# Scan stage of an RWKV block: one transposed product moved behind the next level's first step, and the adaptive weights moved from VectorE to ScalarE and GpSimd

## What is computed

```python
# the scan, per head: S is value x key
S = S * w_t + (S @ a_t) b_t^T + v_t k_t^T ;  y_t = S @ r_t
# the adaptive weights of the second block, which depend on c alone
mod = silu(c) @ ada_w + ada_b          # 1024 x 6144, for sh1, sc1, g1, sh2, sc2, g2
```

## Time and profile before

| | |
|---|---|
| median of 3 runs | 3071.32 us (3067.51 to 3080.73) |
| the profiled execution | 3072.96 us, of which its span (first to last instruction) is 3071.2 us |
| mean granted TensorE clock over the span | 0.981 of full |
| busy over the span | PE 2954.0, PEld 2562.2, DVE 1954.5, ACT 1195.3, POOL 765.9 us |
| the scan | from 242.28 to about 549.5 us in the trace |

### The profile page before, as it was taken

How to read it: one execution, slowest core, us unless ns; L and a number is a source line. 1 busy time by engine, 2 the same in 40 slices (tenths; PEclk the granted TensorE clock), 3 DMA queues, 4 the chain that set the end, 5 groups by cost and what they waited for, 6 DMA issues and landing times.

```text
span 3071.2 us, 48256 instructions
## 1 busy us (share of the span) xinstructions
PE 2954.0 (96%) x19809; PEld 2562.2 (83%) x19809; DVE 1954.5 (64%) x3498; ACT 1195.3 (39%) x1949; POOL 765.9 (25%) x517
## 2 busy tenths in 40 slices
PE   8998888899999999999999999999999999999999
PEld 6776888788888878888787878999999997888887
DVE  5584676633324553332468557798979867878878
ACT  6363332423223342332336333445454543333332
POOL 1010111000000200000012002776767763533422
PEclk9998999999999999999999999999999999999999
DMA  4313222333323323332221122779889899999997
GB/s 125 110 37 98 85 86 94 127 98 97 100 97 117 96 86 99 97 96 96 81 81 36 35 87 82 246 273 320 287 297 312 298 334 368 360 366 343 356 367 257
DMA packets 233371, 539.63 MB, mean 176 GB/s; under 512 B 24816, under 2 KB 91632, under 8 KB 231104
## 3 DMA queue, kind: packets, MB, share of 16 engines
q1 hardware_dynamic: 177280, 375.01, 37.0%
q0 software_dynamic: 37440, 136.36, 12.2%
q10 hardware_dynamic: 18432, 25.17, 2.2%
HBM read 484.02 MB, written 52.46 MB: 175 GB/s over the span
## 4 chain that ended last, share of the span: by engine, by line
PE 82%; DVE 7%; POOL 3%; DMA 3%; ACT 3%; issue 2%; SPq 0%; ACTq 0%; DVEq 0%; POOLq 0%
PE bank L396 23%; PE bank L2942 16%; PE bank L399 16%; PE bank L2511 12%; PE bank L2671 3%; POOL etl L2499 2%; DMA eu<-in_peer_u 2%; PE bank L519 1%; PE bank L811 1%; PE bank L1099 1%; POOL taken L2536 1%; DMA gl<-acts 1%; PE bank L1286 1%; PE bank L1143 1%; PE bank L1168 1%
## 5 line engine op out<-in xcount | busy, mean ns | idle before, releaser
L346 DVE TENSOR_TENSOR wl<-raw,wh 128x1024 fp32r<-128x1024 f32 (+2 forms) x241 | 294.5, 1225 | 643.5 <-ACT wh L331 643.5
L331 ACT CAST wh<-raw 128x1024 fp32r<-128x1024 f32 (+2 forms) x241 | 249.7, 1038 | 657.0 <-PE bank L396 367.4
L2499 POOL TENSOR_TENSOR etl<-eu,eth 128x1024 fp32r<-128x1024 f32 x128 | 316.9, 2478 | 390.5 <-ACT eth L2495 389.3
L2511 PE MATMUL bank<-peerhh,eth 128*128 128x384 f32 x1024 | 349.1, 341 | 10.3 <-POOL etl L2499 9.9
L2511 PE MATMUL bank<-peerhh,etl 128*128 128x384 f32 x1024 | 343.6, 336 | 0.0
L2511 PE MATMUL bank<-peerhl,eth 128*128 128x384 f32 x1024 | 343.4, 335 | 0.0
L2942 PE MATMUL bank<-vsh,coefh 128*128 128x512 f32 x768 | 299.2, 390 | 3.2 <-DVE coefl L3007 2.7
L2942 PE MATMUL bank<-vsh,coefl 128*128 128x512 f32 x768 | 298.8, 389 | 0.0
L2942 PE MATMUL bank<-vsl,coefh 128*128 128x512 f32 x768 | 298.8, 389 | 0.0
L2536 POOL DMA_INDIRECT taken<-in_peer_v,gb x128 | 198.2, 1548 | 310.0 <-DVE y_row L2556 302.8
L2963 ACT CAST vsh<-vb 128x1024 fp32r<-128x1024 f32 x128 | 134.7, 1052 | 193.8 <-PE bank L2942 164.5
(11 more groups left out here) (561 smaller groups left out, 6851.6 us busy)
## 6 DMA issues: line engine op xcount, KB each, us to landing
eu<-in_peer_u SPq DMA_DIRECT2D x128, 512.0 KB
vb<-in_peer_v SPq DMA_DIRECT2D x128, 512.0 KB
raw<-in_ada_w SPq DMA_DIRECT2D x48, 512.0 KB, 4.6
acts<-eg ACTq DMA_DIRECT2D x128, 192.0 KB
coefs<-stage SPq DMA_DIRECT2D x24, 1024.0 KB
gd<-coefs SPq DMA_DIRECT2D x16, 1536.0 KB
gl<-acts SPq DMA_DIRECT2D x128, 192.0 KB
raw<-in_ffn_w_gate SPq DMA_DIRECT2D x44, 512.0 KB, 3.6
```

Source lines behind the costliest of these rows:

```text
L331: act.copy(parts_of(c)[0], raw_of(c)).then_inc(*up("w rounded", c))
L346: dve.tensor_tensor(lo, raw_of(c), hi.bitcast(F32), ALU.subtract).then_inc(*up("w split", c))
L2499: pool.tensor_tensor(Et[j % 3][1], Eu[j % 2], Et[j % 3][0].bitcast(F32), ALU.subtract).then_inc(*up("u split", j))
L2511: t = pe.matmul(b, tb[un][:, k * 128:(k + 1) * 128], peer_h[hn][:, k, 1:4, :], start=k == 0 and i == 0, stop=k == 7 and i == 2)
```

## The change

Four edits, all within the scan.

1. PE's xt step becomes a function of its own. The xt step of half 0 comes after both x steps; that of half 1 comes after the next level's two w steps, ahead of that level's grid product. ACT's copies follow the same order.
2. The products of the adaptive weights go to ACT (`ada_scaled`: 2 per piece, in place in `raw`) and the sums to POOL (`ada_added`: 1 or 2 additions per piece). ACT's are placed one half of a piece after each of levels 1 to 4, and two halves at a time after the low blocks, after the corners, after the next group's first turn, and after the copy of y.
3. On POOL the normalisation of y (`dve_gn`) stands between pieces 6g+1 and 6g+2.
4. The last chunk (ch = 3, g = 6) no longer transposes b and k, which nothing reads there.

```diff
--- before.py
+++ after.py
@@ -1158,6 +1158,9 @@
                 t = pe.matmul(b[side(p), bank, 64 * n:64 * n + 64], part(XTc, w)[at_, c:c + 64],
                               eye(l, w)[at_, cw:cw + 64], start=True, stop=True)
         t.then_inc(*up("scan pe", "x full", g, l, w))
+
+    def pe_level_xt(pe, on_pe, g, l, w):
+        order = CROSS[l - 1] if l > 1 else SIDES[1]
         b, before = banks.take_pair(("xt", g, l, w), ("scan act", "xt new", g, l, w), *([("scan dve", "xt low", g, w)] if l == 5 else []))
         for what in before:
             on_pe.wait_ge(*at(*what))
@@ -1210,7 +1213,7 @@
 
         for g in range(NG):
             ch, gp = divmod(g, 2)
-            if gp == 0:
+            if gp == 0 and ch < 3:
                 for name, src in (("b", aa), ("k", k_)):
                     for half in range(2):
                         b, before = banks.take(("bk", name, ch, half), ("bk", name, ch, half))
@@ -1222,12 +1225,16 @@
             for l in range(1, 6):
                 for w in range(2):
                     pe_level_w(pe, on_pe, g, l, w)
+                if l > 1:
+                    pe_level_xt(pe, on_pe, g, l - 1, 1)
                 if l in TASKS:
                     pe_grids(pe, on_pe, g, TASKS[l])
                 for w in range(2):
                     pe_level_x(pe, on_pe, g, l, w)
+                pe_level_xt(pe, on_pe, g, l, 0)
                 if l in ADAS:
                     total(6 * g + ADAS[l])
+            pe_level_xt(pe, on_pe, g, 5, 1)
             for w in range(2):
                 pe_low(pe, on_pe, g, w)
             b, before = banks.take(("g", g), ("g copied", g))
@@ -1318,6 +1325,24 @@
         for what in DECAYED:
             on_act.wait_ge(*at(*what))
 
+        def xt_new(g, l, w):
+            b = banks.pair(("xt", g, l, w))
+            on_act.wait_ge(*at("scan pe", "xt full", g, l, w))
+            if l < 5:
+                act.copy(part(XTc, w).rearrange("p (b n) -> p b n", b=2), b[:, :, 0:128]).then_inc(
+                    *up("scan act", "xt new", g, l, w))
+            else:
+                act.copy(XTf[0:64, :, 2 * w:2 * w + 2, 0:64], bank_four(b, 0)[0:64]).then_inc(
+                    *up("scan act", "xt new", g, l, w))
+
+        def ada_scaled(n, k):
+            ga, i = divmod(n, 4)
+            c = st.plans["ada", ga][0][2][i]
+            on_act.wait_ge(*at("silu c"))
+            on_act.wait_ge(*at(f"w in {c % 4}", c))
+            act.activation(raw_of(c)[:, k, :], raw_of(c)[:, k, :], ACT.Copy,
+                           scale=silu_c[:, 2 * i + k:2 * i + k + 1]).then_inc(*up("scan act", "ada scaled", n, k))
+
         def squares(g):
             on_act.wait_ge(*at("dve step", "y", g, "centred"))
             act.activation(Sq, Yc, ACT.Square).then_inc(*up("y squares", g))
@@ -1327,28 +1352,29 @@
         on_act.wait_ge(*at("bank full", "bonus", KD - 1))
         for g in range(NG):
             ch, gp = divmod(g, 2)
-            if gp == 0:
+            if gp == 0 and ch < 3:
                 for name, dst in (("b", bkT[ch % 2][0]), ("k", bkT[ch % 2][1])):
                     on_act.wait_ge(*at("bank full", "bk", name, ch, 0))
                     for what in bk_free(ch):
                         on_act.wait_ge(*at(*what))
                     act.copy(dst[:, 0:512], banks["bk", name, ch, 0]).then_inc(*up("bk", name, ch, 0))
             for l in range(1, 6):
+                if l > 1:
+                    xt_new(g, l - 1, 1)
                 for w in range(2):
-                    x, b, rows = banks.pair(("x", g, l, w)), banks.pair(("xt", g, l, w)), slice(0, 128 if l < 5 else 64)
+                    rows = slice(0, 128 if l < 5 else 64)
                     on_act.wait_ge(*at("scan pe", "x full", g, l, w))
-                    act.copy(part(Xc, w).rearrange("p (b n) -> p b n", b=2)[rows], x[rows, :, 0:128]).then_inc(
-                        *up("scan act", "x new", g, l, w))
-                    on_act.wait_ge(*at("scan pe", "xt full", g, l, w))
-                    if l < 5:
-                        act.copy(part(XTc, w).rearrange("p (b n) -> p b n", b=2), b[:, :, 0:128]).then_inc(
-                            *up("scan act", "xt new", g, l, w))
-                    else:
-                        act.copy(XTf[0:64, :, 2 * w:2 * w + 2, 0:64], bank_four(b, 0)[0:64]).then_inc(
-                            *up("scan act", "xt new", g, l, w))
+                    act.copy(part(Xc, w).rearrange("p (b n) -> p b n", b=2)[rows],
+                             banks.pair(("x", g, l, w))[rows, :, 0:128]).then_inc(*up("scan act", "x new", g, l, w))
+                xt_new(g, l, 0)
+                if l < 5:
+                    ada_scaled(6 * g + (l - 1) // 2, (l - 1) % 2)
+            xt_new(g, 5, 1)
             for w in range(2):
                 on_act.wait_ge(*at("scan pe", "low full", g, w))
                 act.copy(part(Vc, w)[64:128], banks["low bank", g, w][64:128, 0:256]).then_inc(*up("scan act", "low", g, w))
+            for k in range(2):
+                ada_scaled(6 * g + 2, k)
             if g:
                 squares(g - 1)
             on_act.wait_ge(*at("g full", g))
@@ -1359,6 +1385,8 @@
                 on_act.wait_ge(*at("scan pe", "corner full", g, w))
                 act.copy(XTf[0:64, :, 2 * w:2 * w + 2, 64:128], four(banks["corner bank", g, w][:, 0:256])[0:64]).then_inc(
                     *up("scan act", "corner", g, w))
+            for k in range(2):
+                ada_scaled(6 * g + 3, k)
             on_act.wait_ge(*at("u full", g))
             if g:
                 on_act.wait_ge(*at("state full", g - 1))
@@ -1366,10 +1394,14 @@
             if g + 1 < NG:
                 for w in range(2):
                     act_first_turned(act, on_act, g + 1, w)
+            for k in range(2):
+                ada_scaled(6 * g + 4, k)
             on_act.wait_ge(*at("y full", g))
             if g:
                 on_act.wait_ge(*at(*normed_v(g - 1)))
             act.copy(Yc, banks["y", g]).then_inc(*up("y copied", g))
+            for k in range(2):
+                ada_scaled(6 * g + 5, k)
         squares(NG - 1)
 
     def dve_grid(dve, on_dve, g, name, q):
@@ -1396,7 +1428,6 @@
         for what in DECAYED:
             on_dve.wait_ge(*at(*what))
         on_dve.wait_ge(*at("bank full", "bonus", KD - 1))
-        on_dve.wait_ge(*at("silu c"))
         on_dve.wait_ge(*at("zeros", "state"))
 
         def grid(g, name, q):
@@ -1404,19 +1435,6 @@
 
         def ada(n):
             ga, i = divmod(n, 4)
-            c = st.plans["ada", ga][0][2][i]
-            acc = accs[ga % 2]
-            on_dve.wait_ge(*at(f"w in {c % 4}", c))
-            for k in range(2):
-                x = silu_c[:, 2 * i + k:2 * i + k + 1]
-                if i + k == 0:
-                    if ga >= 2:
-                        on_dve.wait_ge(*at("bank full", "ada", ga - 2))
-                    t = dve.tensor_scalar(acc, raw_of(c)[:, k, :], x, None, ALU.mult)
-                else:
-                    on_dve.wait_ge(*at("dve step", "ada", ga, 2 * i) if k else at("ada used", c - 1))
-                    t = dve.scalar_tensor_tensor(acc, raw_of(c)[:, k, :], x, acc, ALU.mult, ALU.add)
-                t.then_inc(*(up("ada used", c) if k else up("dve step", "ada", ga, 2 * i)))
             if i == 1 and ga:
                 ada_sum(ga - 1)
 
@@ -1534,8 +1552,28 @@
         for what in DECAYED:
             on_pool.wait_ge(*at(*what))
         pool.memset(f("state", 128, 1024), 0.0).then_inc(*up("zeros", "state"))
-        for g in range(NG - 1):
-            dve_gn(pool, on_pool, up, "v normed pool", g, "pool step")
+
+        def ada_added(n):
+            ga, i = divmod(n, 4)
+            c, acc = st.plans["ada", ga][0][2][i], accs[ga % 2]
+            on_pool.wait_ge(*at("scan act", "ada scaled", n, 1))
+            if i == 0:
+                if ga >= 2:
+                    on_pool.wait_ge(*at("bank full", "ada", ga - 2))
+                pool.tensor_tensor(acc, raw_of(c)[:, 0, :], raw_of(c)[:, 1, :], ALU.add).then_inc(*up("ada used", c))
+                return
+            on_pool.wait_ge(*at("ada used", c - 1))
+            pool.tensor_tensor(acc, acc, raw_of(c)[:, 0, :], ALU.add).then_inc(*up("pool step", "ada", n))
+            on_pool.wait_ge(*at("pool step", "ada", n))
+            pool.tensor_tensor(acc, acc, raw_of(c)[:, 1, :], ALU.add).then_inc(*up("ada used", c))
+
+        for g in range(NG):
+            for n in range(2):
+                ada_added(6 * g + n)
+            if g:
+                dve_gn(pool, on_pool, up, "v normed pool", g - 1, "pool step")
+            for n in range(2, 6):
+                ada_added(6 * g + n)
```

## The result

The changed kernel takes **3089.45 us** (median of 20 runs, 3079.8 to 3106.47); the kernel before, run beside it, 3076.55 (20 runs, 3067.51 to 3091.92). The ratio is 1.0039, 95% interval 1.0023 to 1.0055: about 12 us slower. The forecast was 3070.7 and the range ended at 3083. Of the 18.8 us between forecast and result, 5.2 lie in the base: the forecast was counted from 3071.32, the median of 3 runs of the kernel before, and over 20 runs that kernel has 3076.55. The profiled execution took 3082.37 us, span 3080.6.

The account below looks back on a forecast made before the run. PE, busy for 96% of the span, was taken as the bound, with at most 43.5 us idle in the scan. Terms -4.2 - 1.85 + 4.0 + 1.4 = -0.65 us gave 3070.7 us, range 3059 to 3083.

Parts of the forecast that it names:

- edit 1, order: Levels of the scan: w steps start 0.25 us earlier in levels 2 and 4; 4.2 us won over 8 groups.
- edit 4, transposes: Start of group 6: 16 matmuls leave PE, the next matmul having followed at once; 1.85 us won.
- edits 2 and 3 without waits and late end: Scan: DVE loses some 69 us of work, ACT gains 69 us; both costed at 0 for PE.
- waits for POOL: Between y and state product: PE waits 1.6 us in groups 2 and 4, 0.8 in 6; 4.0 us lost.
- end of the scan: Last piece scaled, added and summed behind the last y, delaying DVE's last bias; 1.4 us lost, bounds 0 and 3.
- The lower bound of the prediction, 0: Edit 1 in the levels: nothing won if the bubbles called "issue" fill the room again.
- at 0, bounds 0 and 1 us: Group 0: ACT's first product may wait for its piece's transfer; costed at 0, PE having stood still 3.03 us there.
- rival 4: Clock falls behind the new waits ahead of the state product in groups 2, 4, 6: +18 us, 3088; 10%.
- Edit 2's load: Scan: 96 products on ACT, some 69 us, lie in ACT's gaps; ACT about 165 us, costed at 0.
- rival 3: DVE and POOL exclude each other when DVE centres y in groups 2, 4, 6: +7.6 us, 3078; 6%.
- Rival 1: The waits for POOL stay hidden because PE reaches the total later: -4.65 us, 3066.7; 12%.
- Rival 2: Clock holds better in the scan through shorter gaps in the levels: -17 us, 3054; 11%.

Follow-up runs that it names:

- e1: Kernel before plus edit 1 alone (new order of the levels); 3087.06 us, ratio 1.0024.
- e7: e6 plus edit 1 (new order), adaptive weights not moved; 3076.51 us, ratio 1.0000.
- e6: Kernel before with edit 4 alone and the turn of the PSUM banks restored at the end of the scan; 3072.46 us, ratio 0.9975.
- e8: e4 with POOL's third piece added ahead of the normalisation and the last piece scaled ahead of the last copy of y; 3071.24 us, ratio 0.9991.
- e12: e8 again, beside the kernel before on another chip; 3073.22 us, ratio 0.9963.
- e9: e8 without edit 1, so the levels in the order of before; 3061.22 us, ratio 0.9942.
- e18: e9 again, on another chip; 3063.48 us, ratio 0.9953.
- e15: e9 with POOL's third piece behind the normalisation again, so PE waits for POOL three times; 3075.51 us, ratio 0.9984.
- e14: e9 with ACT's products of the last piece behind the last copy of y again; 3064.32 us, ratio 0.9961.
- e2: Kernel before plus edits 2 and 3 alone (adaptive weights by ACT and POOL); 3084.93 us, ratio 1.0030.
- e4: Changed kernel plus one line restoring the turn of the PSUM banks at the end of the scan; 3079.62 us, ratio 1.0004.
- e11: The changed kernel measured again, beside the kernel before on another chip; 3092.55 us, ratio 1.0021.
- e17: e15 with six products that nobody reads ahead of PE's wait for POOL in groups 2, 4 and 6; 3064.84 us, ratio 0.9951.

## Why the prediction was wrong, step by step

The forecast summed to -0.65 us; the runs give some +12. The effects read from pairs of ratios, in us (each uncertain by 6 to 10):

| part | forecast | by the runs |
|---|---|---|
| edit 1, order | -4.2 | +8 (e1; e7 - e6; e8, e12 - e9, e18) |
| edit 4, transposes, without the leak | -1.85 | -8 (e6) |
| edits 2 and 3 without waits and late end | 0 | -8 (e9, e18 - e6) |
| waits for POOL | +4.0 | +11 (e15 - e9, e18) |
| end of the scan | +1.4 | +4 (e14 - e9, e18) |
| the leak | none | +4 (five pairs) |
| sum | -0.65 | +11, measured +12 and, again, +6 |

The parts that e2 holds (waits, end, weights) add to +7, where it measured +9; those of e4 (all but the leak) also to +7, where it measured +1. So the parts don't add up to better than their uncertainty.

The step that failed is the conversion of PE's gains and waits into time. The forecast counted each at its own length: 4.2 us won by edit 1, 4.0 lost by the waits for POOL, and nothing for the clock behind them or for the banks behind the scan. The runs show +8 for the first, +11 for the second and some +4 for the leak. Two other parts won 6 and 8 us more than forecast and took much of that back; that the total came out as near the range as it did is luck.

**Edit 1** came about in the levels as described and still won nothing. Group 3, the first products of levels 1 and 4, before:

```profile
361.76 0.69 PE L1143 MATMUL bank<-eyes,AT 64*64 64x64 f32 x32
...
370.88 0.68 PE L1143 MATMUL bank<-x half,AT 64*64 64x64 f32 x32
```

and those of levels 1, 2 and 4 in the changed kernel:

```profile
354.32 0.69 PE L1143 MATMUL bank<-eyes,AT 64*64 64x64 f32 x32
...
357.43 0.69 PE L1143 MATMUL bank<-x half,AT 64*64 64x64 f32 x32 [0.59 <-ACT xt half L1332]
...
362.99 0.69 PE L1143 MATMUL bank<-x half,AT 64*64 64x64 f32 x32 [0.83 <-DVE RB L1413]
```

Level 2 starts 3.11 us after the first product, where it was 3.40 (the earlier trace rows have its start at 365.16); all eight groups of before have 3.4, and all but the last of the changed kernel 3.1. (The wait is put down to ACT's postponed copy, which ends 0.02 us after DVE's mask; it hardly adds to it.) Level 4 starts 0.45 us earlier, as forecast. But from there to the copy of the low block it takes 7.61 us instead of 7.33, so the levels of group 3 took 16.28 us (354.32 to 370.60) against 16.45 (361.76 to 378.21): 0.17 us won, where 0.5 were forecast. The lower bound of the prediction, 0, was for the case that the gaps called issue "fill the room again", and it is this that came: over the scan PE's waits with and without the order are equal (e6 and e7, above). What it hadn't is a price above 0, which all three comparisons in the table show, at a lower mean clock each time.

In group 0 ACT's product, which waits for its piece, stands ahead of the postponed copy:

```profile
249.92 0.72 ACT L1343 ACTIVATE raw<-raw,small 128x512 f32<-128x512 f32 x1 [2.80 <-DMA raw<-in_ada_w]
250.55 0.35 ACT L1332 COPY xt half<-bank 128x256 f32<-128x256 f32 x1
...
251.04 0.60 PE L1158 MATMUL bank<-eyes,xt half 64*64 64x64 f32 x15 [2.08 <-ACT xt half L1332]
```

That was the place costed "at 0, bounds 0 and 1 us" because PE "stood still for 3.03 us there anyway". The copy in the queue behind the product wasn't named, but the price was right: level 3 of group 0 starts 8.61 us after the group's first product here, 8.59 in e1, which has no such products, and 9.01 in the kernel before.

**The waits for POOL** were right in place, number and length: 1.3 us each, 4.0 in all, against 1.6, 1.6 and 0.8. Their price was wrong. I counted the waits' own length and gave the clock's fall behind them to **rival 4** with 10%, at 3088, "from waits of about 3 us on". Waits of 1.3 us were enough for that mechanism. That the changed kernel landed next to its number, at 3089, is luck: rival 4 had +18 us from the waits alone, with 12 us of low clock behind each; the rows have some 4 us behind each, the waits cost 11, and the rest of the way is made of other parts and the higher base. The earlier trace rows had the fall behind a gap, and also one with PE busy all the time, and I let the second speak against the first. The Trainium skill, TensorE: Matmul & The Clock Gate, section "Why this matters for your kernels", asks that a kernel have no long idle gaps between bursts of products if it is to hold its throughput. The rows agree with the direction; they show that waits of 1.3 us already cost, in a stretch that has many other gaps.

**Edit 4** had its instructions counted rightly, and the 1.85 us can't be told apart inside the 8. But its step went by instructions only: that a `take` not made moves every later one was missed. It is the only known part of the loss that lies outside the scan, and the description of the kernel ahead of the prediction even says that banks go in rotation.

**Edit 2's load** was right: outside group 0 PE waited no more than 0.7 us in all for transposed copies behind ACT's products (L1158, above); its one wait of 1.4 us for a copy of X, in group 1, stands in e7 as well (1.1 us), which has no such products. And DVE's two instructions on y take 691 to 693 ns, as before, so rival 3 didn't come. **The end** was right in kind, 1.7 us for 1.4. **Rival 1** fell with the three waits. **Rival 2**, the clock holding better through shorter gaps in the levels, didn't come in the changed kernel (0.88 in the scan of its profile). A better clock is what e9 shows, with the old order: 3061, a mean clock of 0.985, and 0.95 in the scan of its profile where the earlier trace rows have 0.89.

What stays open: why the new order goes with a lower clock (0.980 against 0.981 in e7 and e6, 0.983 against 0.985 in e12 and e9, each by one to two standard errors) though PE's waits in the scan aren't longer in sum. That they lie in other places is all that the traces show; filling those waits wasn't tried. Nor is it shown why taking the transposes out, or the weights off VectorE, wins 8 us each where instructions account for 2 and 0: both kernels show a higher mean clock, and that is as far as the runs go.

## What to carry to other kernels

Price a new wait on TensorE not by its length but by the clock behind it: here 4 us of waits cost some 11, and where useless products filled them the clock stayed up. Count the gain of a shorter level at the end of the stage, not at the step where it arises. And where resources are handed out in turn, compare the whole list of turns before and after; removing a user far ahead can put a wait into code that nobody touched, and one line restores it.

## What the runs showed of the hardware

- The same kernel on the same chip spreads over 36 us (3062.88 to 3098.98), in the other groups of runs over 31 to 45 us. Within a group the time falls with the granted clock, by 2.5 to 2.9 us for 0.001, and the clock accounts for 84 to 93% of the variance. The scan alone takes from 288.2 us (e8, its clock at 0.94) to 320.9 (e2, 0.85) in single profiles. One profile of such a kernel says little about a term of a few microseconds.
- Waits of 1.3 us on TensorE, each between two dense stretches, were followed by the lower clock (0.50) in 14 of 15 places: two of three in the changed kernel, three of three in each of e2, e4, e11 and e15. In the same places without a wait it didn't fall (45 places in 15 traces), and not when the wait was filled with products (e17, three of those 45).
- GpSimd's additions on 128x512 took 1.27 us with a start every 1.35, though GpSimd was busy for 140 us of the scan instead of 37, and ScalarE's products with a scale 0.73 us: both as their nearest rows of before had them.
